# Up-projection of a gated feed-forward as seven block products in two token passes, 2u ahead of 4a

## What is computed

```python
h2 = rmsnorm(x, lp['norm_ffn']) * (1.0 + sc2) + sh2
a, u = jnp.split(h2 @ lp['w_ffn_in'], 2, axis=-1)
x = x + g2 * ((jax.nn.silu(a) * u) @ lp['w_ffn_out'])
```

## Time and profile before

| | us |
|---|---|
| median of 3 runs (3294.55 to 3299.69) | 3295.6 |
| span of the profiled execution | 3299.5 |
| PE busy in it | 3164.7 |
| DVE, ACT, POOL busy | 1489.9, 997.1, 642.8 |
| feed-forward of layer 0, layer 1 (from first to last of its groups) | 788, 789 |

### The profile page before, as it was taken

One profiled execution on the slowest core, in us unless ns is written; L12 is line 12 of the kernel. 1 busy time (PEld: TensorE's weight loads), 2 busy tenths in 40 slices (PEclk: granted clock), 3 DMA queues, 4 the chain that ended last, 5 costly groups with the idle time before them and its releaser, 6 DMA issues. The chain is left out here.

```text
span 3299.5 us, 50698 instructions
## 1 busy us (share of the span) xinstructions
PE 3164.7 (96%) x19758; PEld 2859.2 (87%) x19758; DVE 1489.9 (45%) x2623; ACT 997.1 (30%) x2083; POOL 642.8 (19%) x955
## 2 busy tenths in 40 slices
PE   6999989999999999999999999899999999999999
PEld 5997666768999999999989966666699999999999
DVE  5312656655533344333382045665645443333443
ACT  5222345444311211111152234554434111111111
POOL 2113566520100000000041155663210000000000
PEclk8999999999999999999999999999999999999999
DMA  6415811104011111111123262111310111111101
GB/s 219 140 70 178 251 44 60 36 29 132 26 51 38 38 51 51 51 38 38 39 80 110 96 223 62 54 52 29 111 52 26 53 49 51 38 38 38 51 26 55
DMA packets 189219, 237.15 MB, mean 72 GB/s; under 512 B 18649, under 2 KB 160302, under 8 KB 189070
## 3 DMA queue, kind: packets, MB, share of 16 engines
q1 hardware_dynamic: 134156, 158.44, 14.9%
q10 hardware_dynamic: 44354, 45.25, 4.3%
q0 software_dynamic: 10560, 31.44, 2.7%
HBM read 195.53 MB, written 39.56 MB: 71 GB/s over the span
## 5 line engine op out<-in xcount | busy, mean ns | idle before, releaser
L1588 PE MATMUL banks<-act_split,w_split 128*128 128x384 f32 (+1 forms) x8352 | 1389.7, 327 | 7.6 <-DVE act_split L2351 7.1
L1588 PEld LDWEIGHTS banks<-act_split,w_split 128*128 128x128 f32 x8352 | 1377.9, 188 | 14.7 <-issue 7.0
L1588 PE MATMUL banks<-hidden_split,w_split 128*128 128x384 f32 (+1 forms) x3168 | 527.4, 326 | 0.0
L1588 PEld LDWEIGHTS banks<-hidden_split,w_split 128*128 128x128 f32 x3168 | 522.3, 188 | 0.5
L2409 DVE SCALAR_TENSOR_TENSOR x<-banks,mod,x 128x384 f32<-128x384 f32 (+2 forms) x768 | 353.2, 496 | 188.2 <-PE banks L1588 185.9
L2867 DVE TENSOR_TENSOR hidden_f<-banks,silu_a 128x384 f32<-128x384 f32 x132 | 70.7, 536 | 736.5 <-PE banks L1588 736.5
L1588 PE MATMUL banks<-w_split_tm,act_split 128*128 128x396 f32 (+1 forms) x1728 | 317.2, 344 | 0.0
L1588 PEld LDWEIGHTS banks<-w_split_tm,act_split 128*128 128x128 f32 (+1 forms) x1728 | 300.9, 182 | 13.2 <-issue 4.0
L1552 ACT ACTIVATE w_split<-w_raw 128x2048 fp32r<-128x2048 f32 x60 | 112.5, 1906 | 381.3 <-PE banks L1588 381.3
L1546 ACT ACTIVATE hidden_split<-hidden_f 128x384 fp32r<-128x384 f32 x132 | 67.0, 508 | 519.6 <-DVE hidden_f L2867 519.6
L641 POOL TENSOR_TENSOR norm_sum_n<-norm_sum_n,norm_sq 128x384 f32<-128x384 f32 (+1 forms) x42 | 46.4, 1106 | 790.6 <-ACT norm_sq L961 785.9
(11 more groups left out here) (239 smaller groups left out, 3234.3 us busy)
## 6 DMA issues: line engine op xcount, KB each, us to landing
w_raw<-in_w_ffn_in SPq DMA_DIRECT2D x44, 1024.0 KB, 5.1
w_mod_front<-in_w_mod ACTq DMA_DIRECT2D x50, 512.0 KB, 5.7
w_raw<-in_w_ffn_out SPq DMA_DIRECT2D x22, 1024.0 KB, 4.9
w_mod_third<-in_w_mod ACTq DMA_DIRECT2D x26, 512.0 KB, 5.4
z_token_major<-z_stage POOLq DMA_DIRECT2D x64, 198.0 KB, 2.2
...
w_raw<-in_w_o SPq DMA_DIRECT2D x8, 1024.0 KB, 6.5
```

What stands on the lines that cost most here:

```text
L1588: return T.matmul(out, lhsT, rhs, start=start, stop=stop, skip_group_check=True)
```

## The change

The up-projection of a group is made by Strassen's scheme in Winograd's form, and in two passes over the tokens: `p` 0 takes tokens 0 to 543 through all 11 groups, `p` 1 the other 544, so there are 22 half-groups a layer. In a half-group each of the blocks `a` and `u` is a product of 256 hidden columns, 1024 features and 544 tokens, cut in two in every direction. `W00` to `W11` are quarters of the raw weights (hidden half, feature half; 128 x 512 elements with features four deep), `B11` to `B22` quarters of the activations of 272 tokens. With S1 = W10+W11, S2 = S1-W00, S3 = W00-W10, S4 = W01-S2 and T1 = B12-B11, T2 = B22-T1, T3 = B22-B12, T4 = B21-T2 the seven products are 1: W00 B11, 2: W01 B21, 3: S4 B22, 4: W11 T4, 5: S1 T1, 6: S2 T2, 7: S3 T3, each of 12 matmuls of 272 columns. 6, 7 and 4 are accumulated onto product 1's bank; ACT copies the bank's content between them (`p1a`, `u2a`, `u3a`; `p1u`, `u2u`, `u3u`) into `PU`. DVE adds what is missing (`c11a`, `c22a`, `c12a` and for u), ACT gates, POOL multiplies three of the four hidden quarters (`m11u`, `m22u`, `m12u`), DVE the fourth, ACT and DVE split them (`g`, `h`). 16 down blocks of six matmuls of 272 columns follow.

The weight operands lie in seven sets (`w_set`; 0 W00, 1 S1, 2 S2, 3 W01, 4 S3, 5 W11, 6 S4). Sets 0 to 5 serve both blocks in turn, so the up block's set is free to be written when the gate block's product has read it. ACT makes each high part (`w_high`), DVE the low parts l0 to l4 (`w_low`), POOL the four sums S1 to S4 and the low parts l5 and l6 (`w_step`). The down weights are split in four pieces, f0 to f3 (`out_high`, `out_low`). The weights of every group are loaded twice, once in each pass. The products stand in the order of `PE_ORDER`; in it the up block's product 2 (2u) stands ahead of the gate block's product 4 (4a). The sets of the activations, the norm's scaling and the second pass's T sums are made in hooks of the first, second, eleventh and twelfth half-groups, the next layer's first norm in the twelfth and last. These five (0, 1, 10, 11, 21) are written out, the 17 others are in two loops. The blocks of the projection ahead (`WO_SEQ`) stand in another order, with the same matmuls. Where `h_parts` splits tokens, the residual adds of pass 1 are of 208 and 64 columns.

```diff
+HALF, PASSN = 272, 544
+PRODUCT = {"1": (0, 0, 0, 0, True, "B11"), "5": (1, 0, 1, 2, True, "T1"), "6": (2, 4, 1, 0, False, "T2"),
+           "2": (3, 4, 0, 1, True, "B21"), "7": (4, 0, 2, 0, False, "T3"), "4": (5, 4, 2, 0, False, "T4"),
+           "3": (6, 0, 3, 2, False, "B22")}
+READ_BY = {p[0]: k for k, p in PRODUCT.items()}
+SET_OF = {p[5]: (p[1], p[2], k) for k, p in PRODUCT.items()}
+PE_ORDER = ["1a", "5a", "6a", "2a", "7a", "1u", "2u", "4a", "3a", "6u", "7u", "5u", "4u", "3u"]
+BANK_FREE = {"1a": ("ffn_dve", -1, "x12"), "5a": ("ffn_dve", -1, "x14"), "6a": ("ffn_act", 0, "p1a"),
+             "2a": ("ffn_dve", -1, "x13"), "7a": ("ffn_act", 0, "u2a"), "1u": ("ffn_dve", -1, "x11"),
+             "4a": ("ffn_act", 0, "u3a"), "3a": ("ffn_dve", 0, "c22a"), "6u": ("ffn_act", 0, "p1u"),
+             "2u": ("ffn_dve", -1, "x15"), "7u": ("ffn_act", 0, "u2u"), "5u": ("ffn_dve", -1, "x10"),
+             "4u": ("ffn_act", 0, "u3u"), "3u": ("ffn_dve", 0, "c22u")}
+OUT_ROT = [0, 1, 2, 4, 5, 3]
...
+    WS1 = place("w_sets_first", [P, 4, 2, 512], F32R, [w_at + SLOT * 8, w_end])
+    WS2 = place("w_sets_last", [P, 4, 2, 512], F32R, [w_at + SLOT * 16, w_end])
...
+    def w_set(i, b):
+        return WS1[:, i] if i < 4 else WS2[:, i - 4] if i < 6 else WS2[:, 2 + (b == "u")]
...
+                def next_raw(turn, i):
+                    wait(sp, "fwa_dve", turn - 1, "l4")
+                    wait(sp, "fwa_pool", turn - 1, "l6")
+                    load_raw(l, 16, w_f1_v[l][:, :, bass.ds(i * GROUP, GROUP)], 8)
+                    wait(sp, "fwo_dve", turn - 1, "f3")
+                    load_raw(l, 18, w_f2_v[l][:, bass.ds(i * 2, 2), :], 2)
+                    wait(sp, "fwu_dve", turn - 1, "l4")
+                    wait(sp, "fwu_pool", turn - 1, "l6")
+                    load_raw(l, 17, w_f1_v[l][:, :, bass.ds(i * GROUP + D_FF, GROUP)], 8)
...
+                def w_step(b, turn, name, first=False):
+                    s = st(f"fw{b}_pool")
+                    i = int(name[1])
+                    if name[0] == "l":
+                        wait(pool, f"fw{b}_act", turn, f"h{i}")
+                        src = w_quarter(b, 1, 1) if i == 5 else w_sum(6, b)
+                        hi = w_set(i, b)[:, 0].bitcast(F32).rearrange("p (k c) -> p k c", k=4)
+                        out = w_set(i, b)[:, 1].rearrange("p (k c) -> p k c", k=4)
+                        s.done(V.tensor_tensor(out, src, hi, ALU.subtract), name)
+                        return
+                    to = {1: 1, 2: 2, 3: 4, 4: 6}[i]
+                    pool.wait_ge(raw_ld[1 + (b == "u")], w_ready(b, turn))
+                    set_free(pool, b, turn, to)
+                    if first:
+                        wait(pool, "wo_pe", l, "o11" if to < 4 else "o21")
+                    if i == 2:
+                        wait(pool, f"fw{b}_pool", turn, "S1")
+                    elif i == 4:
+                        wait(pool, f"fw{b}_pool", turn, "S2")
+                    x, y, op = {1: (w_quarter(b, 1, 0), w_quarter(b, 1, 1), ALU.add), 2: (w_sum(1, b), w_quarter(b, 0, 0), ALU.subtract),
+                                3: (w_quarter(b, 0, 0), w_quarter(b, 1, 0), ALU.subtract),
+                                4: (w_quarter(b, 0, 1), w_sum(2, b), ALU.subtract)}[i]
+                    s.done(V.tensor_tensor(w_sum(to, b), x, y, op), name)
...
+                def group(g, hook=lambda name: None, last=False):
+                    s = st("ffn_pool")
+
+                    def times(name, i, j):
+                        wait(pool, "ffn_dve", g, f"c{name}u")
+                        wait(pool, "ffn_act", g, f"s{name}a")
+                        s.done(V.tensor_tensor(SIL[:, i], SIL[:, i], PU[:, j], ALU.mult), f"m{name}u")
+                        hook(f"m{name}u")
+
+                    for name in ("S1", "S2", "S4", "S3", "l5", "l6"):
+                        w_step("u", g, name)
+                    hook("sums")
+                    times("11", 0, 0)
+                    times("22", 3, 2)
+                    if not last:
+                        for name in ("S1", "S2"):
+                            w_step("a", g + 1, name)
+                    times("12", 1, 1)
+                    if not last:
+                        for name in ("S4", "S3", "l5", "l6"):
+                            w_step("a", g + 1, name)
+                    hook("end")
...
+                    def kept(name, product, i, reader):
+                        bank = 3 if name[-1] == "u" else 0
+                        wait(act, "ffn_pe", g, product)
+                        wait(act, *reader)
+                        s.done(S.activation(PU[:, i], ps[bank][:, 0:HALF], ACT.Copy), name)
...
+                    kept("p1a", "1a", 0, ("ffn_pool", g - 1, "m11u"))
+                    out_high(g, 0)
+                    out_high(g, 1)
+                    w_high("u", g, 0)
+                    kept("u2a", "6a", 1, ("ffn_pool", g - 1, "m12u"))
+                    out_high(g, 2)
+                    out_high(g, 3)
+                    gated("11", 0)
+                    w_high("u", g, 3)
+                    kept("u3a", "7a", 2, ("ffn_pool", g - 1, "m22u"))
+                    w_high("u", g, 1)
+                    w_high("u", g, 2)
+                    gated("22", 3)
+                    kept("p1u", "1u", 0, ("ffn_dve", g, "c11a"))
+                    w_high("u", g, 4)
+                    wait(act, "ffn_pe", g, "4a")
+                    wait(act, "ffn_dve", g - 1, "h21")
+                    s.done(S.activation(SIL[:, 2], ps[0][:, 0:HALF], ACT.Silu), "s21a")
+                    w_high("u", g, 6)
+                    w_high("u", g, 5)
+                    gated("12", 1)
...
+                    kept("u2u", "6u", 1, ("ffn_dve", g, "c12a"))
+                    if not last:
+                        w_high("a", g + 1, 0)
+                    kept("u3u", "7u", 2, ("ffn_dve", g, "c22a"))
+                    hidden("11", 0, ("ffn_pool", g, "m11u"))
+                    if not last:
+                        w_high("a", g + 1, 3)
+                    hidden("21", 2, ("ffn_dve", g, "m21u"))
+                    hidden("22", 3, ("ffn_pool", g, "m22u"))
+                    hidden("12", 1, ("ffn_pool", g, "m12u"))
+                    if not last:
+                        for i in (1, 2, 6, 4, 5):
+                            w_high("a", g + 1, i)
+                            hook(f"a{i}")
...
+                def group(g, hook=lambda name: None, sets=None):
+                    for name in PE_ORDER:
+                        b = name[1]
+                        i, row, place_, bank, start, part = PRODUCT[name[0]]
+                        wait(pe, f"fw{b}_pool" if i >= 5 else f"fw{b}_dve", g, f"l{i}")
+                        if sets is not None and b == "a":
+                            wait(pe, "hs_dve", sets, f"l{part}")
+                        wait(pe, BANK_FREE[name][0], g + BANK_FREE[name][1] if BANK_FREE[name][1] else g, BANK_FREE[name][2])
+                        out = ps[bank + (3 if b == "u" else 0)][:, 0:HALF]
+                        w, h = w_set(i, b), [h_set(part, xa) for xa in range(2)]
+                        for k in range(4):
+                            for j, (wa, xa) in enumerate(PASSES):
+                                ins = mm(out, w[:, wa, P * k:P * k + P], h[xa][:, k], start and k == 0 and j == 0, k == 3 and j == 2)
+                        s.done(ins, name)
+                        hook(name)
+                    wait(pe, "fwo_dve", g, "f3")
+                    for q in range(16):
+                        ch, d = divmod(q, KT8)
+                        if d == 0:
+                            wait(pe, "ffn_dve", g, "h12" if ch else "h21")
+                        if q == 4:
+                            wait(pe, "ffn_dve", g, "c12u")
+                        elif q >= 6:
+                            wait(pe, "ffn_dve", g, f"x{q - 6}")
+                        for k in range(2):
+                            for j, (wa, xa) in enumerate(PASSES):
+                                ins = mm(ps[OUT_ROT[q % 6]][:, 0:HALF], WO2[:, wa, 1024 * k + P * d:1024 * k + P * d + P],
+                                         HID[:, xa, k, HALF * ch:HALF * ch + HALF], k == 0 and j == 0, k == 1 and j == 2)
+                        s.done(ins, f"x{q}")
+                        hook(f"x{q}")
...
+                with pe.Fori(2, NGROUP - 1) as i:
+                    group(g0 + i)
+                group(g0 + NGROUP - 1)
+                group(g0 + NGROUP, again, 2 * l + 1)
+                settle(pe)
+                with pe.Fori(NGROUP + 1, 2 * NGROUP - 1) as i:
+                    group(g0 + i)
+                group(g0 + 2 * NGROUP - 1, ending)
...
+                def h_low(p, name):
+                    turn = 2 * l + p
+                    wait(dve, "hs_act", turn, name)
+                    if name in ("B11", "T1"):
+                        wait(dve, "hs_pool", turn, "T1" if name == "B11" else "T2")
```

(39 more changed lines are left out.)

683 lines of the change are left out of this document (465 added, 218 removed).

## The result

The changed kernel takes 3587.0 us (3584.3 to 3592.4) against 3297.6 for the kernel before in the same comparison: ratio 1.088, 95% interval 1.0865 to 1.0896. That is 289 us slower where 203 were forecast. The profiled execution's span is 3586.5 us; against 3299.5 it is +287.0, and that is the difference that the traces have to explain.

A forecast was written before the change was run, and what follows sets the result against it. PE's own work was taken to bound the kernel. Half-groups 1690 us, set-up 70 and layer starts 6, less the old 1563, gave +203 on 3295.6: 3499 us; forecast range 3420 to 3565, wider range 3320 to 3620.

The forecast's parts named there:

- the rival of the clock: Loop half-groups: PE's clock falls to half after 2u's wait, 1.7 us each in four fifths, +60 us, 3560 us; chance 0.17.
- What bounds the kernel before: Feed-forward groups: only PE's own work counts, 71.05 us a group, 1563 us for 22; DVE and ACT are covered.
- The matmul's price: All half-groups: a 272-column matmul takes 126.7 ns, 264 of them 33.44 us; -91.6 us over 22 groups.
- Seven products cost as eight: Half-groups: a 272-column matmul costs 146.7 ns, 38.7 us of PE work, about 39.4 us a half-group, 3540 us; chance 0.05.
- The shared path and the timetable: Half-group: DVE's two-SBUF-input operations and POOL's take turns; waits add to 5.0 us, 38.4 us a half-group, +127 us.
- the lock: DVE instructions with two SBUF inputs and POOL ones exclude each other; 24.2 of 33.4 us held in turn per half-group.
- the cover holds: Half-groups: DVE finishes f1 to f3 by 7.1 us, 2u does not wait; 34.4 us each, 3266 us; chance 0.18.
- the last one: The last-listed rival, matmuls of 272 columns at 146.7 ns in the half-groups: 3540 us; chance 0.05.
- The half-group without the clock: One half-group with PE's clock at full: 33.4 us of PE work plus 5.0 us of waits, 38.4 us.
- the first pair might go DVE's way: Half-group's first DVE subtraction and POOL sum: if DVE goes first, c11a is at 9.0 us, the half-group 37.3 us.
- The set-up: Five written-out half-groups a layer: scalings, sums and norm cost 35 us a layer, plus 3 at the start.
- 2u ahead of 4a: PE's product order: both hang on c11a, so with 4a first the half-group would be 0.4 us shorter.

The follow-up runs named there:

- e5_both_orders: Changed kernel with the same instructions in another order on PE (2u between 6u and 7u) and on DVE: 3315.9 us, ratio 1.0042.
- e2: Changed kernel with DVE making the low parts f1, f2, f3 behind l4u instead of ahead of c11a: 3401.4 us, ratio 1.0303.
- e3: Changed kernel with POOL's four weight sums per block cut to 128 of 512 elements, raw weights read instead: 3371.1 us, ratio 1.0205.

## Why the prediction was right, and where it was short

The direction and the mechanism held; the measured 3587 lies inside the stated 3320 to 3620, but outside the forecast's own 3420 to 3565 and nearest to the rival of the clock (3560, chance 0.17). By its steps:

- **What bounds the kernel before**: right. PE's own work decided; in the window above it is busy in 787.2 of 790.5 us.
- **The matmul's price**: 126.7 ns expected from the line through two rows, 127.0 measured in e5_both_orders. The interval of an isolated matmul that the Trainium skill gives ("TensorE: Matmul & The Clock Gate", section "Back-to-back issue gap"), by which the half-group would have been an estimated 30.6 us, doesn't hold for these matmuls: 33.52 us were measured. "Seven products cost as eight" falls.
- **The shared path and the timetable**: right, and shown by e2 and e3. Expected c11a at 10.1 us and waits of 3.2, 0.7, 0.3 and 0.8; measured 10.14 and 3.18, 0.58, 0.34 and 0.71. The four subtractions behind f0 take 1.7 to 1.8 us each, the PSUM sums 0.43. Two sentences of the prediction on it were wrong, without harm: the 0.55 us at 659.60 hardly stand beside a fill, since POOL's ended at 659.63 and what followed was a copy of two partitions; and without the lock the sum would have been that of the rival "the cover holds", not of the last one. What shows the stretch are e2 and e3.
- **The half-group without the clock**: 38.4 expected, 38.84 measured. Beside a wait PE also loses some 0.1 us at each restart (12 matmuls take 1.77 us behind a wait and 1.68 elsewhere), and four restarts are 0.4. Over 44 half-groups this is 19 us that the sum lacked.
- **The clock**: the term that was put among the rivals and belonged into the sum. It fell in 12 of layer 0's 17 loop half-groups and in 13 of layer 1's, together three quarters (four fifths were guessed). In 18 of these 25 that costs 1.5 us (1.7 guessed), in the other seven, where it was granted at half for longer, about 2.5. A loop half-group of layer 0 is 40.14 us on average, 1.3 more than 38.84; a little of that is a wait at the first one's start. For all 44 half-groups it is 57 us, of which 44 lie in the 34 of the loops; the rest is only counted here and not with the set-up. The argument against it, that the first pair might go DVE's way and the wait be 2 us, was not borne out: it was 3.18 in every one. With this term the forecast would have been 3556, and with the restarts 3575.
- **The set-up**: 35 + 3 us a layer above the loops' half-groups, less nothing for what the kernel before spends. Measured: 928.9 less 22 times 40.14 are 45.8 us, and the kernel before has 8.9 of its own above its eleven groups, so 37 net. The sum came out by luck, as its parts were wrong: the start costs 25 us a layer and not 3, the rest some 21 and not 35. The clock is in these too: in layer 0's part it was granted at half for 102 us, of which the loops hold 46, and the kernel before has 3. No run separates what it costs there from the waits.
- **Between the layers**: 15 us, and 4 fewer ahead of the first layer's part. The sum had no term of its own for them; the prediction named the next layer's norm only in the upper end of the set-up's cost.
- **2u ahead of 4a**: 0.4 us a half-group expected, 0.53 measured. What was missed is that this half microsecond also decides how often the clock falls: together 45 us.

In sum: 203 expected, + 57 for the clock (by the average above), + 19 for the restarts, + 11 between the layers and ahead of them, - 2 for the set-up: 288, against 287.0 by the spans.

The rival "the cover holds" was off for the kernel as written, but its mechanism is real: with three subtractions moved (e2) the wait at 2u is gone, and its 34.4 us a half-group are what e3 nearly shows (34.86). It gave 3266 with 20 us of set-up; e5, at 33.5 us a half-group, took 3316. The rival had the set-up too cheap.
